# Cross attention: keys and half of the queries turned inside the queries' product, one modulation piece moved ahead of the NSA attention

## What is computed

```
def cross_attention(h, m, w_q, w_kv, w_o):
    q = (h @ w_q).reshape(Bn, S, 4, 256)
    kv = (m @ w_kv).reshape(Bn, 256, 2, 4, 256)
    k, v = kv[:, :, 0], kv[:, :, 1]
    s = einsum('bshd,bmhd->bhsm', q, k) * 256 ** -0.5
    o = einsum('bhsm,bmhd->bshd', softmax(s), v).reshape(Bn, S, 1024)
    return o @ w_o
...
c_act = silu(c)
for l in range(2):
    mod = c_act @ ada_w[l] + ada_b[l]        # 9 parts of 1024: shift, scale, gate, three times
```

## Time and profile before

| what | value |
|---|---|
| time, median of 3 runs | 1509.71 us (1508.74 to 1511.02) |
| time of the profiled execution | 1511.61 us |
| its span | 1509.9 us |
| mean granted clock of PE | 0.989 |
| busy: PE, PEld, DVE, ACT, POOL | 1454.7, 1198.5, 1053.9, 731.1, 77.4 us |
| chain that ended last: PE, DVE, ACT | 84%, 8%, 4% |

### The profile page before, as it was taken

One profiled execution on the slowest core, in us unless ns is written; L12 is line 12 of the kernel. 1 busy time (PEld: TensorE's weight loads), 2 busy tenths in 40 slices (PEclk: granted clock), 3 DMA queues, 4 the chain that ended last, 5 costly groups with the idle time before them and its releaser, 6 DMA issues.

```text
span 1509.9 us, 18760 instructions
## 1 busy us (share of the span) xinstructions
PE 1454.7 (96%) x7206; PEld 1198.5 (79%) x7206; DVE 1053.9 (70%) x1428; ACT 731.1 (48%) x1108; POOL 77.4 (5%) x133
## 2 busy tenths in 40 slices
PE   8998989999999999998999999999999988999998
PEld 7886877888877888887778888788888767788886
DVE  4787555877777777766587777877677678685544
ACT  6546545444455443364464343543435765554342
POOL 7200000000000000010000000000000000000000
PEclk9999999999999999999999999999999999999999
DMA  8851434797756977634368887588883610576560
GB/s 283 298 187 38 168 112 168 242 310 256 278 187 226 312 261 268 226 123 158 114 235 301 271 271 266 193 302 271 278 288 125 216 33 1 181 251 207 184 209 28
DMA packets 189087, 314.21 MB, mean 208 GB/s; under 512 B 6896, under 2 KB 100440, under 8 KB 189000
## 3 DMA queue, kind: packets, MB, share of 16 engines
q1 hardware_dynamic: 148800, 232.87, 46.6%
q10 hardware_dynamic: 38408, 75.65, 14.1%
q0 software_dynamic: 1792, 4.51, 0.9%
HBM read 311.92 MB, written 1.07 MB: 207 GB/s over the span
## 4 chain that ended last, share of the span: by engine, by line
PE 84%; DVE 8%; ACT 4%; issue 2%; DMA 1%; POOL 0%; ACTq 0%; POOLq 0%; DVEq 0%
PE ps L1189 25%; PE ps L1191 24%; PE ps L1190 24%; PE ps L1198 5%; PE ps L1521 2%; PE ps L1336 2%; PE ps L1467 1%; DVE wlo L1145 1%; DVE rmax L2364 1%; DVE tmp L2048 1%; ACT sp L1889 1%; ACT whi L1126 1%; DVE wide L1145 0%; DMA raw<-in_nsa_w_out 0%; ACT pT L1897 0%
## 5 line engine op out<-in xcount | busy, mean ns | idle before, releaser
L1145 DVE TENSOR_TENSOR wlo<-raw,whi 128x2048 fp32r<-128x2048 f32 (+2 forms) x168 | 381.5, 2274 | 111.3 <-ACT whi L1126 110.9
L1189 PE MATMUL ps<-whi,aT 128*128 128x512 f32 (+3 forms) x1000 | 399.0, 399 | 6.0 <-DVE aTl L2036 4.0
L1191 PE MATMUL ps<-wlo,aT 128*128 128x512 f32 (+3 forms) x1000 | 387.7, 388 | 0.0
L1190 PE MATMUL ps<-whi,aTl 128*128 128x512 f32 (+3 forms) x1000 | 386.6, 387 | 0.0
L1126 ACT ACTIVATE whi<-raw 128x2048 fp32r<-128x2048 f32 (+2 forms) x166 | 314.0, 1895 | 31.2 <-PE ps L1191 24.3
L1189 PEld LDWEIGHTS ps<-whi,aT 128*128 128x128 f32 x1000 | 187.9, 188 | 48.9 <-issue 9.2
L1191 PEld LDWEIGHTS ps<-wlo,aT 128*128 128x128 f32 x1000 | 187.7, 188 | 39.4
L1190 PEld LDWEIGHTS ps<-whi,aTl 128*128 128x128 f32 x1000 | 188.3, 188 | 34.0
L1831 ACT ACTIVATE hT<-ps 128x256 fp32r<-128x256 f32 (+1 forms) x102 | 42.2, 413 | 342.8 <-PE ps L1198 342.8
L1189 PE MATMUL ps<-whi,hT 128*128 128x512 f32 (+1 forms) x364 | 141.3, 390 | 1.4 <-ACT z L1806 1.4
L1191 PE MATMUL ps<-wlo,hT 128*128 128x512 f32 (+1 forms) x364 | 138.4, 382 | 0.0
(11 more groups left out here) (271 smaller groups left out, 2021.1 us busy)
## 6 DMA issues: line engine op xcount, KB each, us to landing
raw<-in_ff_w SPq DMA_DIRECT2D x176, 512.0 KB, 4.9
raw<-in_ff_w SPq DMA_DIRECT2D x44, 1024.0 KB, 5.2
qT<-in_ada_w ACTq DMA_DIRECT2D x36, 1024.0 KB, 6.4
pT<-in_ada_w ACTq DMA_DIRECT2D x36, 1024.0 KB, 7.4
raw<-in_w_up SPq DMA_DIRECT2D x16, 1024.0 KB, 6.0
raw<-in_w_down SPq DMA_DIRECT2D x16, 1024.0 KB, 5.8
raw<-in_w_in SPq DMA_DIRECT2D x9, 1024.0 KB, 8.9
raw<-in_w_ckv SPq DMA_DIRECT2D x8, 1024.0 KB, 5.1
```

Of the source, the lines that this page charges most:

```text
L1145: dve.tensor_tensor(lo_of(u), raw_of(u), hi_of(u).bitcast(F32), ALU.subtract).then_inc(w_lo, 1)
L1189: pe.matmul(out_ap, hi, w, start=start, stop=False)
L1190: pe.matmul(out_ap, lo, w, start=False, stop=False)
L1191: return pe.matmul(out_ap, hi, wl, start=False, stop=stop)
```

## The change

- The cross attention's eight turns no longer stand behind the product. Keys 0 and 1 are turned behind unit 1 of w_cq, keys 2 and 3 and queries 0 and 1 behind unit 2. Queries 2 and 3 are turned at the end of step 0 of the attention, both emptied by DVE, and the scores of group 2 wait for them. The turning list for the cross attention takes which queries and keys it does, keys first.
- No modulation piece is started behind the first attention or in w_cq (`ada_until(0)`).
- From the MLA attention to the NSA attention a piece is started down to room 5 (`ada_least`), elsewhere down to 6 as before.

```diff
--- before.py
+++ after.py
@@ -103,6 +103,7 @@
         self.ada_todo = []
         self.ada_n = 0
         self.ada_open = []
+        self.ada_least = 6
         self.ada_t = None
         self.ada_done = {}
         self.ada_closed = 0
@@ -370,7 +371,7 @@
             m["age"] += 1
             out += self.ada_step(m)
         latest = self.ada_open[-1] if self.ada_open else None
-        if self.ada_todo and self.ada_room >= 6 and (latest is None or latest["age"] >= self.ada_every[self.ada_n % 2]):
+        if self.ada_todo and self.ada_room >= self.ada_least and (latest is None or latest["age"] >= self.ada_every[self.ada_n % 2]):
             out += self.ada_start()
         self.ada_room -= 1
         return out
@@ -621,11 +622,21 @@
     p.linear(A["w_ckv"][0], D, 2 * D, "zc", "w_ckv", side=after_in, lhs="ha", inner={6: first_head})
     attend("first", list(heads["first"]["turned"]), A["w_out"][0], None,
            {0: first_rest, 4: diff(0)[0], 5: diff(0)[1], 6: diff(1)[0], 7: diff_end, 8: early(0), 9: early(1, 0), 10: first_end}, 4, late)
-    p.ada_until(6)
+    p.ada_until(0)
     p.edge(p.out_rest(out[0]), ("prm", G_CROSS), eps=1e-5)
-    p.linear(A["w_cq"][0], D, D, "z", "w_cq", flush=3)
-    p.turned("qk_cross", 8, ["A", "D"] * 4)
-    attend("cross", list(p.keys_turned), A["w_co"][0], None, {4: first_half(), 5: early(0), 6: rest_then_early})
+    cross, late = [], {}
+
+    def cross_turn(qs, ks, who):
+        p.turned("qk_cross", len(qs) + len(ks), list(who), qs=qs, ks=ks)
+        cross.extend(p.keys_turned)
+
+    def cross_rest():
+        p.turned("qk_cross", 2, "D", qs=(2, 3), ks=())
+        late[2] = p.keys_turned
+
+    p.linear(A["w_cq"][0], D, D, "z", "w_cq", flush=3,
+             inner={1: lambda: cross_turn((), (0, 1), "AD"), 2: lambda: cross_turn((0, 1), (2, 3), "ADAD")})
+    attend("cross", cross, A["w_co"][0], None, {0: cross_rest, 4: first_half(), 5: early(0), 6: rest_then_early}, late=late)
     p.ada_every = (4,4)
     p.ada_until(65)
     acc = p.out_rest(out[0])
@@ -680,6 +691,7 @@
             attend("mla", turned, A["hy_w_out_2"][0], (p.n_gates + 1, 1.0),
                    {1: lambda: p.gate(layer, 5), 4: conv_last, 5: early(0), 6: rest_then_early})
             p.ada_until(69)
+            p.ada_least = 5
             acc = p.out_rest(out[0])
             p.wide, p.zc_left = True, (p.groups[-1]["fill"], 1)
         else:
@@ -731,6 +743,7 @@
 
             attend("nsa", turned, A["nsa_w_out_2"][0], (p.n_gates + 1, 1.0), {2: lambda: p.gate(layer, 5), 21: finish, 22: finish_rest})
             p.ada_until(35)
+            p.ada_least = 6
             acc = p.out_rest(out[0])
         p.edge(acc, ("mod", 2), (layer, 6), mod=(layer, 2))
         acc = p.mlp("swiglu", A["ff_w13_2"][layer, 1], A["ff_w2_2"][layer, 1], N2, HB2, (layer, 8, 0.5), f"ff{layer}1")
@@ -1049,10 +1062,10 @@
                     dst.append([(kz[HD * c:HD * c + HD, 4 + 4 * r + c:4 + 4 * r + c + 3:2, :], HD * c, HD, 0, 512)
                                 for c in range(2)])
             elif kind == "qk_cross":
-                for r in range(4):
+                for r in st["ks"]:
+                    pair(zc, 256 * r, kz[:, 2 * r:2 * r + 2, :])
+                for r in st["qs"]:
                     pair(z, 256 * r, qT[:, 2 * r:2 * r + 2, :])
-                for r in range(4):
-                    pair(zc, 256 * r, kz[:, 2 * r:2 * r + 2, :])
             elif kind in ("q_mla", "k_mla"):
                 src, to = (z, qT) if kind == "q_mla" else (kfull, kz)
                 for r in range(4):
```

## The result

The changed kernel takes 1518.53 us in the median of 6 runs (1515.11 to 1521.27), the kernel before 1510.02 us in 6: ratio 1.0057, 95% interval 1.0040 to 1.0073. Five more runs, made later beside other kernels, have the median 1516.14 (ratio 1.0047, 1.0034 to 1.0060). With the single execution of a second profile (1516.61) the twelve have the median 1517.3. The forecast was 1515.4. The profiled execution took 1515.89 us with a span of 1514.1, 4.2 above the span of before.

The account below looks back on a forecast made before the run. PE, with 84% of the chain, was taken to bound the kernel, losing time only where it stands still or does side work. Gain 4.1 and loss 9.8 gave +5.7 on the 1509.71 us median: 1515.4 us, range 1510.5 to 1519.

Parts of the forecast that it names:

- rival A: The forecast itself: stall of about 7 us ahead of cmp_hid with a clock fall, 1513 to 1517.5 us; chance 0.60.
- The gain in the cross stage: w_cq and cross attention: scores 5.6 us earlier, part given back by late query turns; 4.1 us won, bounds 3.0 and 5.6.
- PE's turns inside: w_cq: waits and turns of 1.7 and 2.3 us plus 0.1 for changes of matmul kind; scores 4.1 us after 203.76.
- No value for the freed DVE time and loads in w_cq: w_cq: the removed piece's 2 MB of loads and 6 us of DVE bring nothing beyond the 1.16 + 0.95 already counted.
- The walk of DVE's queue: nsa_in: DVE in order ends terms 4 to 7 at 1194.5; cmp_hid starts at 1195.4 instead of 1186.86, 8.6 us lost.
- The loads are not late: nsa_in: extra piece's loads issued near 1168.2 and 1174, taking 6.4 and 7.4 us, against needs at 1176.2 and 1189.
- Clock, 2.0 us: Behind the wait ahead of cmp_hid: PE at half speed for 3.4 to 5.6 us, costing 1.7 to 2.8; 2.0 taken.
- 0.8 us back at the query turn: At 1199.90, where PE had waited 1.34 us for DVE: with PE 8 us later DVE is ahead, 0.8 us back.
- The bounds of the loss: nsa_in and cmp_hid: loss 9.8 us, from 7.2 (no clock fall, chain 0.6 shorter) to 11.5.
- B: Rival B, nsa_in: flush costs only 2.1 us as DVE's gaps swallow the terms; net -2.0, 1507.7 us; chance 0.14.
- D: Rival D, ahead of cmp_hid: stall 2 us less and no clock fall; net +1.7, 1511.4 us; chance 0.16.
- C: Rival C: half speed throughout cmp_hid and only 3 us gained in the attention; 1520.3 us; chance 0.10.

Follow-up runs that it names:

- the move alone: Kernel before with only the modulation piece moved (none in w_cq, one more in nsa_in), turns left outside the product: 1518.98 us, ratio 1.0067.
- the kernel kept busy: Changed kernel with 40 dummy matmuls on PE in the wait ahead of the extra piece's sum: 1513.07 us, ratio 1.0025.
- the profile with small loads: Changed kernel with the extra piece loading an eighth of its columns, the rest stale: 1517.34 us, ratio 1.0057; profiled execution 1521.09 us.

## Why the prediction was right, step by step

- **Direction and size.** +5.7 us was forecast; the medians say +8.5 and +6.1, the two stretches together +7.0 in the first profile, +5.6 and +6.1 in the others. What happened is rival A, the forecast, and the move alone carries the loss; but one premise held only by luck, and part of one term may be chance (below). The first median, 1518.5, lies beyond A's 1517.5, the second within.
- **The gain**. Key turns with a wait for z: 0.8 us forecast, 0.69 measured. Scores directly behind the product: yes. Third scores 5.6 us behind the first, named by DVE's qT: 5.48. The gain in the cross stage: 4.1 forecast, 4.4 measured. The term that was too large is the one for PE's turns inside (4.1 us, measured 3.9). But the 9.74 us taken out of the kernel before hold some 3.4 us at half clock, and none of the eleven other profiles has any in A: with the same eight turns in the same place, the move alone took 6.40 us from the first turn to the scores (203.69 to 210.09), and the kernel before 7.47 (206.03 to 213.50). There is no second profile of the kernel before, so some 1.1 of the 4.4 us may be chance.
- **No value for the freed DVE time and loads in w_cq**: the product ran the same length within 0.1 us in both, apart from the turns (second edge turn to scores: 22.9 us with 3.9 of turns, against 18.9 to the end of the product of before).
- **The walk of DVE's queue.** Term 7's end was forecast 8.6 - 0.95 = 7.6 us behind the old start of cmp_hid; from the rows turn to the piece's sum the walk has 19.7 us (1174.80 to 1194.5), and the three profiles have 19.4, 20.4 and 21.4, the shortest being the one without a late load. The idle was 7.24 there, and 7.25 with the move alone, against "about 7". This is the step that carried the forecast.
- **"The loads are not late"** was wrong in the first and the third profile, and in the second it held by luck. The first load took 12.0 us from its issue, DVE waited 1.93 us for it, and the idle was 9.24; the second and third profile have 9.6 and 11.0 us, with DVE waiting 0 and 0.91. I had taken the median of 36 loads, 6.4 us, while loads of nsa_in and of cmp_hid's weights were in flight; the window 1166 to 1184 of the trace before would have shown the DMA share at 0.71. The second error went the other way: I had the load issued behind the high split, and ACT's queue issued it ahead of it, 2.0 us earlier:

```profile
1159.87 0.37 ACTq L1795 DMA_DIRECT2D qT<-in_ada_w  x1
1159.92 1.91 ACT L1139 ACTIVATE whi<-raw 128x2048 fp32r<-128x2048 f32 x1
```

  Issued where the forecast had it, 8.0 us ahead of its use, a load of 9.6 to 12.0 us would have been 1.6 to 4.0 us late in every profile. The term mis-sized is the landing; what it added to the loss was 0 to 2 us.
- **Clock, 2.0 us**: 2.2 to 2.8 by the comparison with the kernel kept busy. In the three profiles PE worked 4.6, 6.0 and 5.0 us at half clock behind the wait (from the start of the piece's sum to the end of the half clock), where 3.4 to 5.6 were forecast. "No half clock in 204 to 214" held. The Trainium skill ("TensorE: Matmul & The Clock Gate", HAM oscillation) counts half of the throttled time as the penalty. Stretch B agrees if only the time in which PE worked is counted: half of 4.6 to 6.0 is 2.3 to 3.0. The clock was at half for 10.2 us in each of the three, about half of it inside the wait, and half of the whole would be too much.
- **0.8 us back at the query turn**: 1.34 of idle became 0.31, 1.0 back.
- **The bounds of the loss**, 7.2 to 11.5: the terms given add up to 10.6 for the upper one (8.6 - 0.8 + 2.8), and what makes up the other 0.9 isn't said. B lost 10.0, 10.5 and 11.4 us in the three profiles; the last is within the bound only by this unexplained part.
- The rivals: B needed the terms to end before 1188 on the old clock; they ended at 1194.2 in the profile without a late load. D needed a short stall; it was not short. C's time was reached by the two longest runs (1521), which have no profile; in none of the three profiles was all of cmp_hid at half clock, and the gain in A was full.

What stays open: why the changed kernel's runs spread over 6 us. The granted clock of its runs falls from 0.989 to 0.985 as the time rises, and the profile with small loads, of an execution of 1521 us, has more half clock behind the query turn (0.90 against 0.95 in 1204 to 1302). Whether the long wait makes later stretches more frequent, or whether this is chance, was not settled.

## What to carry to other kernels

Work moved off one stall must be followed to where it lands: the piece started at unit 1 of nsa_in, so half of its terms fell into the same unit as its flush, ahead of a product that had no slack on DVE's queue, and 2.5 us saved in one place cost 10 in the other. Before moving work, look whether the order can be changed around it: the turns could go ahead of the flush with the piece left in place, with all of the gain in A (28.31 us against 28.39). Where a helper waits for "the last fill", name the fill that is read; the 0.69 us stood in one place or another in each version until this was done. And where an engine is kept busy through a wait, end the filling before the wait ends.

## What was not expected of the hardware

- A load of 1 MB that takes 6.4 us in the median took 9.5 to 12.0 us at this place in six profiles (12.0, 9.6 and 11.0 in three executions of the changed kernel). With an eighth of the bytes it still took 7.2.
- Half clock comes and goes between executions of the same program. The windows of the three profiles of the changed kernel near their start, in order:

```profile
12.00:20.00 8.00, 7.99 (x44) 7.14 (x42) 6.44 (x12) 6.95 (x14) 5.23 (x11) 0.79 1.03 315
12.00:20.00 8.00, 7.33 (x44) 6.08 (x45) 6.85 (x12) 7.05 (x15) 5.28 (x11) 1.00 1.03 327
12.00:20.00 8.00, 7.84 (x43) 6.99 (x43) 6.41 (x11) 6.95 (x15) 5.47 (x11) 0.79 1.04 331
```

- An idle wait of 7 to 9 us costs more than its length: the work behind it took 2.2 to 2.8 us longer than with PE busy on 40 useless matmuls in it, and by the medians the kernel with them was 3.1 to 5.5 us faster, although they overran the wait by 1.6 us.
